# Two-layer streaming encoder on one core: RWKV's output norm by tile, layer vectors loaded early, feed-forward weights in a ring of four, root first, products of constants on TensorE

## The chip, the core and the metric

The kernel runs on one core of a Trainium2 chip. Its engines are TensorE (PE, matrix products), VectorE (DVE), ScalarE (ACT), GpSimd (POOL) and SyncE (SP, which issues the transfers). The metric is the time of one execution on the device, in microseconds; lower is better. TensorE's clock has two levels here, 1.2 and 2.4 GHz; the profile's column PEclk is the granted share, 0.50 and 1.00.

## The reference, cut

Two layers over 528 tokens (16 meta tokens and 512) of width 1024. A layer is: half-step feed-forward (width 2816), three token mixers side by side (RWKV-7, mLSTM, sparse attention) with a gated merge, second half-step feed-forward. Each has an RMS norm in front and behind.

The second piece below is from `_rwkv7_mixer`, behind its scan.

```python
def _rms_norm(x, g):
    xf = x.astype(jnp.float32)
    y = xf * lax.rsqrt(jnp.mean(xf * xf, axis=-1, keepdims=True) + NORM_EPS)
    return (y * g.astype(jnp.float32)).astype(x.dtype)

def _swiglu(x, w_in, w_out):
    gate, up = jnp.split(x @ w_in, 2, axis=-1)
    return (jax.nn.silu(gate) * up) @ w_out
...
    mean = jnp.mean(y, axis=-1, keepdims=True)
    var = jnp.mean((y - mean) ** 2, axis=-1, keepdims=True)
    y = (y - mean) * lax.rsqrt(var + RW_GN_EPS)
    y = y * gn_gain.astype(f32).reshape(RW_HEADS, RW_HEAD) + gn_bias.astype(f32).reshape(RW_HEADS, RW_HEAD)
    y = y + jnp.sum(r_h * k_h * r_k.astype(f32), axis=-1, keepdims=True) * v_h
    return (y.reshape(bsz, t_len, BRANCH_W) * gate.astype(f32)).astype(p.dtype)
...
    for l in range(DEPTH):
        g = norm_gain[l]
        h = h + 0.5 * _rms_norm(_swiglu(_rms_norm(h, g[0]), ffn_w_in[l, 0], ffn_w_out[l, 0]), g[1])
        u = _rms_norm(h, g[2])
        ...
        h = h + _rms_norm(mixed, g[3])
        h = h + 0.5 * _rms_norm(_swiglu(_rms_norm(h, g[4]), ffn_w_in[l, 1], ffn_w_out[l, 1]), g[5])
```

## The kernel before

Activations stand transposed: feature tiles of 128 partitions by T = 528 tokens (`h` is the residual, KD = 8 tiles; `fo` the output of the last sub-layer, 8 tiles). Two halves of H2 = 264 tokens fill a pair of PSUM banks. An exact product in f32r is three matmuls (`exact`, L141 to L143): weights and activations are split into a high and a low part, high by high, low by high, high by low. The split of weights is made on the chip: ACT copies W to `W_high` (L150), POOL subtracts (`W_low`, L156).

The program is a sequence of phases, each a block of one instruction stream per engine, with all semaphores cleared between two; the streams are ordered by hand with semaphores. Each layer of a loop runs: `phase_params` (13 small transfers of the layer's vectors, two transposes, one copy to `prm`), feed-forward 0, RWKV, sparse attention, mLSTM, merge, feed-forward 1. Behind both layers come a last normalisation (`phase_post_norm`) and the output.

A phase behind a sub-layer begins with a **lead** (class `Lead`). It does the post norm of the sub-layer before, the residual and the sums for the next norm:

- `tensor_post`: column sums of the squares `ssq` over 128 partitions, as matmuls with the squares as weights and one column of `ones` (L355; f32, so each is two instructions of the trace: 20 rows); `factor` on DVE (L381 to L384) turns sums into reciprocals, `root` on ACT (L329) takes the square root, `spread_out` (L362) spreads the factors over partitions on PE.
- for each of 8 tiles k: DVE scales `fo` (L400) and adds it to `h` (L401), ACT makes `u_high` (L338) and the squares (L341), DVE makes `u_low` (L395); PE does the products of tile k for the first two weight tiles (12 matmuls) and the column sums of the squares (L355, 10 rows).
- a second `factor`, `root`, `spread_out`, and the copy to `rs` (L412), by which the feed-forward scales its outputs.

In RWKV's phase (`later` false) the products wait for the second factor: the scaled `h` is made behind it (L423, L348, L417), so that no product lies between the sums.

The feed-forward (`phase_ffn`) has two weight buffers of 8 blocks (128 x 1024). Tile (i, s) is 48 matmuls: gate and up for two hidden tiles each i, s = 0 to 3, PSUM pair s. A buffer is split again when PE is through with the tile before the last (`tile_done`). DVE takes tiles out of PSUM (L603, L608), multiplies by ACT's Silu (L572) and splits the result (L616, L618). The second half of the phase, 8 output tiles of 22 blocks, goes through the same buffers in 24 units. ACT and DVE put out each output tile and its squares (`Out`, L469, L470, L478).

RWKV's output norm is the last block of `phase_rwkv` (L1301 to L1352). It goes step by step over all four tiles of y: sums, mean off, squares, sums of squares, root, `widen` (four DVE copies, L813) and spread, scale, gain and bias, bonus, gate.

## Time and profile before

| | us |
|---|---|
| median of 3 runs | 3931.65 (3928.18 to 3960.33) |
| profiled execution, its own time | 3944.31 |
| its span | 3942.5 |
| TensorE busy | 3576.1, 91% |
| mean granted clock of TensorE | 0.934 |

The page of the profile lists busy time per engine. The view of stretches gives, for a piece of the span, busy time per engine and the granted clock. The timeline lists instructions in order, equal ones merged into one row with their count, and in brackets how long the engine was idle before and what ended it. PE lists a matmul from start to modelled end, so the pitch of a row of matmuls is its length by its count.

### The profile page before, as it was taken

How to read it: one execution, taken by the hardware profiler on the slowest of the kernel's cores; microseconds unless marked ns; L12 is line 12 of the kernel's file. 1: busy time of each engine (PE TensorE's matmuls, PEld its weight loads, DVE VectorE, ACT ScalarE, POOL GpSimd, SP SyncE). 2: the span in 40 equal slices, each digit the busy share in tenths (PEclk: the TensorE clock that was granted, in tenths of full speed). 3: DMA queues.
4: the chain of work that ended last, by engine and by line, in shares of the span. 5: the costliest groups of instructions: out<-in, count | busy, mean ns of one | idle time of the engine just before them, and what ended most of it. 6: DMA issues, size and time to landing. Idle time of an engine off the chain costs nothing. (4 is left out here: it accounts for less than half of the span.)

```text
span 3942.5 us, 76414 instructions
## 1 busy us (share of the span) xinstructions
PE 3576.1 (91%) x32360; PEld 3360.8 (85%) x32360; DVE 1567.9 (40%) x2554; ACT 1066.0 (27%) x1830; POOL 1053.0 (27%) x576
## 2 busy tenths in 40 slices
PE   6999999887979898999979998988789789989998
PEld 5999898775758798999979998987667678989997
DVE  3442244444764123443134413344457631234422
ACT  2222252112453112222222223421125521132221
POOL 2443234110002112344324442341100112124442
PEclk9999899997999898999979998999889889989998
DMA  1333222001101331233223332210011103213332
GB/s 55 91 90 91 70 61 53 3 3 35 49 17 35 81 81 54 75 90 88 78 61 90 90 90 57 69 34 3 2 49 41 35 13 98 73 54 91 90 91 70
DMA packets 458793, 236.77 MB, mean 60 GB/s; under 512 B 15230, under 2 KB 456844, under 8 KB 458524
## 3 DMA queue, kind: packets, MB, share of 16 engines
q1 hardware_dynamic: 458524, 232.90, 21.3%
q8 instruction: 203, 3.33, 0.4%
q14 instruction: 66, 0.54, 0.0%
HBM read 230.50 MB, written 2.10 MB: 59 GB/s over the span
## 5 line engine op out<-in xcount | busy, mean ns | idle before, releaser
L141 PE MATMUL PS<-u_high,W_high 128*128 128x264 f32 x3328 | 965.8, 290 | 46.3 <-POOL W_low L665 23.6
L142 PE MATMUL PS<-u_low,W_high 128*128 128x264 f32 x3328 | 956.3, 287 | 0.0
L143 PE MATMUL PS<-u_high,W_low 128*128 128x264 f32 x3328 | 955.9, 287 | 0.0
L156 POOL TENSOR_TENSOR W_low<-W,W_high 128x1024 fp32r<-128x1024 f32 (+1 forms) x272 | 632.6, 2326 | 1086.4 <-ACT W_high L150 1086.4
L141 PEld LDWEIGHTS PS<-u_high,W_high 128*128 128x128 f32 x3328 | 640.2, 192 | 48.2 <-POOL W_low L665 23.8
L142 PEld LDWEIGHTS PS<-u_low,W_high 128*128 128x128 f32 x3328 | 641.4, 193 | 0.5
L143 PEld LDWEIGHTS PS<-u_high,W_low 128*128 128x128 f32 x3328 | 638.0, 192 | 0.0
L150 ACT ACTIVATE W_high<-W 128x1024 fp32r<-128x1024 f32 (+1 forms) x272 | 281.6, 1036 | 1126.9 <-PE PS L143 1114.7
L141 PE MATMUL PS<-u_high,dW_high 128*128 128x264 f32 (+1 forms) x1536 | 466.5, 304 | 19.3 <-POOL dW_low L1416 7.9
L1416 POOL TENSOR_TENSOR dW_low<-dW,dW_high 128x512 fp32r<-128x512 f32 x128 | 206.5, 1620 | 947.2 <-ACT dW_high L1411 947.0
L142 PE MATMUL PS<-u_low,dW_high 128*128 128x264 f32 (+1 forms) x1536 | 442.9, 288 | 0.0
L143 PE MATMUL PS<-u_high,dW_low 128*128 128x264 f32 (+1 forms) x1536 | 442.8, 288 | 0.0
L142 PE MATMUL PS<-hidden_low,W_high 128*128 128x264 f32 x1408 | 401.0, 285 | 0.0
L143 PE MATMUL PS<-hidden_high,W_low 128*128 128x264 f32 x1408 | 399.2, 284 | 0.0
L141 PE MATMUL PS<-hidden_high,W_high 128*128 128x264 f32 x1408 | 398.9, 283 | 0.0
L141 PEld LDWEIGHTS PS<-u_high,dW_high 128*128 128x128 f32 (+1 forms) x1536 | 296.4, 193 | 36.4 <-issue 21.6
L142 PEld LDWEIGHTS PS<-u_low,dW_high 128*128 128x128 f32 (+1 forms) x1536 | 296.6, 193 | 1.9
L143 PEld LDWEIGHTS PS<-u_high,dW_low 128*128 128x128 f32 (+1 forms) x1536 | 294.8, 192 | 0.0
L478 DVE TENSOR_TENSOR ssq<-ssq 128x528 f32<-128x528 f32 x36 | 89.5, 2487 | 443.6 <-ACT ssq L469 443.6
L141 PEld LDWEIGHTS PS<-hidden_high,W_high 128*128 128x128 f32 x1408 | 265.3, 188 | 0.0
L143 PEld LDWEIGHTS PS<-hidden_high,W_low 128*128 128x128 f32 x1408 | 265.0, 188 | 0.0
L142 PEld LDWEIGHTS PS<-hidden_low,W_high 128*128 128x128 f32 x1408 | 264.3, 188 | 0.0
(339 smaller groups left out, 5403.3 us busy)
## 6 DMA issues: line engine op xcount, KB each, us to landing
W<-in_ffn_w_in SPq DMA_DIRECT2D x176, 512.0 KB, 4.0
dW<-in_w_in SPq DMA_DIRECT2D x188, 256.0 KB, 2.9
W<-in_ffn_w_out SPq DMA_DIRECT2D x64, 512.0 KB, 4.0
W<-in_w_in SPq DMA_DIRECT2D x32, 512.0 KB, 5.4
W<-in_ffn_w_out SPq DMA_DIRECT2D x32, 384.0 KB, 3.5
W_branch<-in_w_branch SPq DMA_DIRECT2D x16, 768.0 KB, 5.1
W<-in_w_out SPq DMA_DIRECT2D x16, 512.0 KB, 4.2
xt<-in_x SPq DMA_DIRECT2D x4, 512.0 KB
```

The source lines that it names most:

```text
L141: nc.tensor.matmul(dst, wh, xh, start=first, stop=False)
L142: nc.tensor.matmul(dst, wh, xl, start=False, stop=False)
L143: return nc.tensor.matmul(dst, wl, xh, start=False, stop=final)
L150: nc.scalar.activation(WH[:, w, 0:k], W[:, w, 0:k], ACT.Copy).then_inc(S("high"), 1)
L156: g.tensor_tensor(WL[:, w, 0:k], W[:, w, 0:k], WH[:, w, 0:k].bitcast(F32), ALU.subtract).then_inc(S("split"), 1)
L478: nc.vector.tensor_tensor(ssq[:, 2], ssq[:, 2] if m > 1 else ssq[:, 0], ssq[:, m % 2], ALU.add).then_inc(S("added"), 1)
L1416: g.tensor_tensor(self.WL[:, r], self.W[:, r], self.WH[:, r].bitcast(F32), ALU.subtract).then_inc(S("d_split"), 1)
```

## The change

1. **Layer vectors.** `phase_params` is gone. A class `Params` issues the 13 transfers within `phase_start` (layer 0) and within feed-forward 1 (the next layer), behind its first eight weight loads on SP; PE transposes them and DVE copies them to `prm` at the end of that phase.
2. **Root first.** ACT takes the square root of a constant at the start of each lead, which puts the table load there; DVE's `memset` of `rq` waits for it. The first weight splits stand behind the root, not ahead of it.
3. **Sums.** Column sums of `Lead` use 64 columns of ones, not 1. In the feed-forward the sums of the eight squares are `ones` by squares (2 x 264 columns), so that they arrive spread over the partitions; reciprocal and root are taken on the 128 x 528 tile `rs`. PE waits only until DVE has read the sums (`sums_read`).
4. **Products of constants.** `occupy` (ones by ones, 128 columns, to a bank not in use): 4 behind the first sums, 12 (feed-forward) or 8 (RWKV) behind the spread, 1 behind each sum of RWKV's lead and 4 behind the last, 8 behind RWKV's second spread, 7 at the end of feed-forward 0 and of the merge.
5. **Ring of four.** The feed-forward's weights go through four buffers of 4 blocks (128 x 512): 88 units for the first half of the phase, 48 for the second, where 44 and 24 were.
6. **RWKV's output norm by tile.** Subtraction of the mean in one step from PSUM, squares, bonus, spread and gates interleaved tile by tile; `wide` and its copies are gone (the spread reads `rq` broadcast to 64 columns, two halves). Gain with bonus, and bias with gate, are each one operation.
7. Two `memset` of RWKV's `s3` go from DVE to POOL.

```diff
+        class Params:
...
+            def load(self, sp, l):
+                pa, pb = self.pa, self.pb
+                come = S("params_come")
+                sp.dma_start(pa[0:48, :], norm_gain[ds(l, 1)].rearrange("a g (k p) -> (a g k) p", p=P)).then_inc(come, 16)
...
+            def turn(self, pe, bank):
+                pe.wait_ge(S("params_come"), 13 * 16)
+                nc.tensor.transpose(bank[:, 0:G_MU], self.pa[0:G_MU, :], ident[0:G_MU, 0:G_MU])
+                n = G_END - G_MU
+                nc.tensor.transpose(bank[:, G_MU:G_END], self.pb[0:n, :], ident[0:n, 0:n]
+                                    ).then_inc(S("params_turned"), 1)
+            def out(self, v, bank):
+                v.wait_ge(S("params_turned"), 1)
+                nc.vector.tensor_copy(prm[:], bank[:, 0:G_END]).then_inc(S("params"), 1)
...
+                    firstp.load(sp, 0)
...
+                    pe.wait_ge(ev["dve_to_pe"], KD - 3)
+                    firstp.turn(pe, PS[:, 0])
...
+                nc.scalar.activation(self.rq[:, 0], ones[:, 0:8], ACT.Sqrt).then_inc(S("table"), 1)
                 self.root(act, 0)
+                if between:
+                    between(act, None)
...
-                self.root(act, 1)
-                if not self.later:
+                if self.later:
+                    act.wait_ge(S("recip"), 2)
+                    nc.scalar.activation(rs[:], rs[:], ACT.Sqrt).then_inc(S("rs"), 1)
...
-                    ins = nc.tensor.matmul(self.sums[0:n, j:j + 1], src[:, t0:t0 + n], ones[:, 0:1],
+                    ins = nc.tensor.matmul(self.sums[0:n, 64 * j:64 * j + 64], src[:, t0:t0 + n], ones[:, 0:64],
...
+                for _ in range(count):
+                    nc.tensor.matmul(self.idle, ones[:], ones[:], start=True, stop=True)
+
             def tensor_post(self, pe):
                 self.column_sums(ssq[:, 2], True, False)
                 self.column_sums(ssq[:, 1], False, True).then_inc(S("summed"), 1)
+                self.occupy(pe, 4)
                 self.spread_out(pe, 0)
+                self.occupy(pe, 12 if self.later else 8 if self.pre is not None else 0)
...
-                self.column_sums(self.ring[k % 2], k == 0, k == KD - 1).then_inc(S("h_summed"), 1)
+                if not self.later:
+                    self.column_sums(self.ring[k % 2], k == 0, k == KD - 1).then_inc(S("h_summed"), 1)
+                    self.occupy(pe, 1 if k < KD - 1 else 4)
+                    return
+                for a in range(2):
+                    last = nc.tensor.matmul(self.wide_sums[:, a], ones[:], self.ring[k % 2][:, a * H2:(a + 1) * H2],
+                                            start=k == 0, stop=k == KD - 1)
+                last.then_inc(S("h_summed"), 1)
...
             def vector(self, v):
                 own = Chain(v, S("norm_own"))
+                v.wait_ge(S("table"), 1)
                 own(nc.vector.memset(self.rq[:], 1.0))
...
+                if self.later:
+                    own(nc.vector.tensor_scalar(halves(rs[:]), self.wide_sums, 1.0 / D_MODEL, EPS, ALU.mult, ALU.add))
+                    v.sem_inc(S("sums_read"), 1)
+                    nc.vector.reciprocal(rs[:], rs[:]).then_inc(S("recip"), 1)
+                    return
                 self.factor(v, own, 1)
                 v.wait_ge(S("spread"), 2)
-                if self.later:
-                    nc.vector.tensor_copy(rs[:], self.spread).then_inc(S("rs"), 1)
-                    return
...
-                W, WH, WL = weight_buffers(st, KD)
+                R = 4
+                W, WH, WL = (sb(st, n, [P, R, 4, P], dt) for n, dt in (("W", F32), ("W_high", F32R), ("W_low", F32R)))
...
+                PARTS = tuple((k0, min(4, KF - k0)) for k0 in range(0, KF, 4))
+                first = [(t, k0) for k0 in (0, 4) for t in range(2)] + [(t, k0) for t in (2, 3) for k0 in (0, 4)]
...
+                        if nextp:
+                            nextp.load(sp, sp.snap(1 - l))
...
+                                for q in range(2):
+                                    load(8 * i + 2 * s + q, (2 * s + q) % R, wi[:, 4 * q:4 * q + 4, ds(c, P)])
...
-                        pe.wait_ge(S("split"), 4)
+                                n = 2 * (k // 4) + s
+                                if k % 4 == 0:
+                                    pe.wait_ge(S("split"), n + 1 + R)
+                                product(s, n, k % 4, k)
                             lead.tensor_square(pe, k)
-                        lead.spread_out(pe, 1)
                         pe.sem_inc(dve_evac, 4)
+                        pe.wait_ge(S("sums_read"), 1)
                         tile(0, 2)
-                        pe.wait_ge(S("rs"), 1)
...
+                            last.then_inc(S("unit_done"), 1)
+                        if nextp:
+                            pe.wait_ge(S("out_put"), KD - 3)
+                            nextp.turn(pe, PS[:, 0])
+                        else:
+                            pe.wait_ge(S("out_put"), KD - 3)
+                            lead.occupy(pe, 7)
...
-                        for s in range(2):
-                            high_part(act, s, 16, W, WH, s, KD)
-                        lead.scalar(act)
-                        high_part(act, 2, 32, W, WH, 0, KD)
+                        def first_high(act, k):
+                            for n in {None: (0, 1), 0: (2,), 1: (3,), 5: (4,), 6: (5,), 7: (6,)}.get(k, ()):
+                                high(n, n // R, n % R, 4)
+
+                        lead.scalar(act, first_high)
+                        high(7, 1, 3, 4)
                         silu(0, 0)
-                        high_part(act, 3, 32, W, WH, 1, KD)
...
+                        if nextp:
+                            v.wait_ge(S("gs"), 1)
+                            nextp.out(v, PS[:, 0])
...
+                    g.memset(s3[:], 1.0).then_inc(S("starts"), 1)
-                    own(nc.vector.memset(s3[:], 1.0))
...
                     lead.spread_out(pe, 1)
+                    lead.occupy(pe, 8)
                     dense.leading_pair(pe, S("u_low"))
...
+                    def bonus_out(m):
+                        v.wait_ge(S("bonus"), m + 1)
+                        nc.vector.tensor_tensor(halves(s1[:, m]), pair(B_PAIR[m]), halves(v_[:, m]), ALU.mult
+                                                ).then_inc(S("bonus_out"), 1)
+
+                    def scaled(m):
+                        v.wait_ge(S("var_spread"), m + 1)
+                        nc.vector.tensor_tensor(y[:, m], y[:, m], spread(S_PAIR[m]), ALU.mult
+                                                ).then_inc(S("scaled"), 1)
+
+                    def joined(m):
+                        v.wait_ge(S("scaled"), m + 1)
+                        v.wait_ge(S("bonus_out"), m + 1)
+                        stt(out=y[:, m], in0=y[:, m], scalar=col(G_GG, m), in1=s1[:, m], op0=ALU.mult, op1=ALU.add
+                            ).then_inc(S("joined"), 1)
+
+                    def gated(m):
+                        v.wait_ge(S("joined"), m + 1)
+                        v.wait_ge(S("gates"), m + 1)
+                        stt(out=halves(y[:, m]), in0=halves(y[:, m]), scalar=col(G_GB, m), in1=pair(G_PAIR[m]),
+                            op0=ALU.add, op1=ALU.mult).then_inc(S("gated"), 1)
...
+                        v.wait_ge(S("sum_y"), m + 1)
+                        stt(out=halves(y[:, m]), in0=pair(m), scalar=-1.0 / 64, in1=halves(y[:, m]),
+                            op0=ALU.mult, op1=ALU.add).then_inc(S("centred"), 1)
...
+                    bonus_out(0)
+                    bonus_out(1)
+                    scaled(0)
+                    bonus_out(2)
+                    joined(0)
+                    bonus_out(3)
+                    gated(0)
+                    for m in range(1, 4):
+                        scaled(m)
+                        joined(m)
+                        gated(m)
...
+                    def spread_out(m):
+                        for j, (t0, n) in enumerate(ST_):
+                            for b in range(2):
+                                c = 8 * j + 2 * m + b
+                                last = nc.tensor.matmul(spread(S_PAIR[m])[64 * b:64 * b + 64, t0:t0 + n],
+                                                        rq[0:n, c:c + 1].broadcast_to([n, 64]), ident[0:n, 0:n],
+                                                        start=True, stop=True)
...
+                        sums(y[:, m], half_ones[:], m, "sum_y")
+                    for m in range(4):
+                        squares(m)
+                    bonus(0)
+                    bonus(1)
+                    pe.wait_ge(S("var_rsqrt"), 1)
+                    spread_out(0)
+                    pe.wait_ge(S("bonus_out"), 1)
+                    bonus(2)
+                    pe.wait_ge(S("bonus_out"), 2)
+                    bonus(3)
+                    gates(0)
+                    pe.wait_ge(S("bonus_out"), 3)
+                    spread_out(1)
+                    pe.wait_ge(S("bonus_out"), 4)
+                    gates(1)
+                    for m in (2, 3):
+                        pe.wait_ge(S("scaled"), m - 1)
+                        spread_out(m)
+                        pe.wait_ge(S("gated"), m - 1)
+                        gates(m)
...
-            run(phase_params, l)
```

ACT at the start of a feed-forward, before (`hid` are the squares, the branches at phase starts left out):

```order
L150 ACT_TABLE_LOAD
L150 ACTIVATE W_high<-W 128x1024 x2
L329 ACT_TABLE_LOAD
L329 ACTIVATE rq<-rq 128x8
L338 ACTIVATE u_high<-h,prm 128x528
L341 ACTIVATE hid<-h 128x528
```

And in the change:

```order
L322 ACT_TABLE_LOAD
L322 ACTIVATE rq<-ones 128x8
L319 ACTIVATE rq<-rq 128x8
L614 ACTIVATE W_high<-W 128x512 x2
L331 ACTIVATE u_high<-h,prm 128x528
L334 ACTIVATE hid<-h 128x528
L614 ACTIVATE W_high<-W 128x512
```

The table for the root is loaded ahead of everything, the root comes ahead of the splits, and these are half as wide.

PE at the start of a feed-forward before, from the sums of the post norm to the first products:

```order
L355 MATMUL PS<-ones,ssq 128x1 x4
L355 MATMUL PS<-ones,ssq 16x1
L355 MATMUL PS<-ones,ssq 128x1 x4
L355 MATMUL PS<-ones,ssq 16x1
L362 MATMUL PS<-ident,rq 128x128 x4
L362 MATMUL PS<-ident,rq 128x16
L141 MATMUL PS<-u_high,W_high 128x264
L142 MATMUL PS<-u_low,W_high 128x264
```

Further on, the last products of tile k = 0, its sums and the first products of k = 1:

```order
L142 MATMUL PS<-u_low,W_high 128x264
L143 MATMUL PS<-u_high,W_low 128x264
L355 MATMUL PS<-ones,hid 128x1 x4
L355 MATMUL PS<-ones,hid 16x1
L141 MATMUL PS<-u_high,W_high 128x264
L142 MATMUL PS<-u_low,W_high 128x264
```

In the change, the same two pieces:

```order
L351 MATMUL PS<-ones,ssq 128x64 x4
L351 MATMUL PS<-ones,ssq 16x64
L368 MATMUL PS<-ones 128x128 x4
L358 MATMUL PS<-ident,rq 128x128 x4
L358 MATMUL PS<-ident,rq 128x16
L368 MATMUL PS<-ones 128x128 x12
L141 MATMUL PS<-u_high,W_high 128x264
L142 MATMUL PS<-u_low,W_high 128x264
```

```order
L141 MATMUL PS<-u_high,W_high 128x264
L142 MATMUL PS<-u_low,W_high 128x264
L143 MATMUL PS<-u_high,W_low 128x264
L384 MATMUL PS<-hid,ones 128x264 x2
L141 MATMUL PS<-u_high,W_high 128x264
L142 MATMUL PS<-u_low,W_high 128x264
```

The constants stand between sums and spread and between spread and products; the ten narrow sums of a tile are two wide matmuls.

PE in RWKV's output norm before, from the spread of tiles 2 and 3 to its end (`gup` are the gate's weights):

```order
L187 MATMUL PS<-ident,wide 128x16
L187 MATMUL PS<-ident,wide 128x128 x4
L187 MATMUL PS<-ident,wide 128x16
L1351 MATMUL PS<-rw_s_1,half_ones 128x264 x8
L1351 MATMUL PS<-pj_rw,gup 128x264 x8
```

And in the change, from the bonus sums of tiles 0 and 1 to the gates of tile 1:

```order
L1430 MATMUL PS<-rw_s_1,half_ones 128x264 x4
L1450 MATMUL PS<-ident,rw_rq 64x128 x8
L1450 MATMUL PS<-ident,rw_rq 64x16 x2
L1430 MATMUL PS<-rw_s_1,half_ones 128x264 x4
L1430 MATMUL PS<-pj_rw,gup 128x264 x2
L1450 MATMUL PS<-ident,rw_rq 64x128 x8
L1450 MATMUL PS<-ident,rw_rq 64x16 x2
L1430 MATMUL PS<-pj_rw,gup 128x264 x2
```

The spread of tile 0 no longer waits for a widened copy, and bonus sums and gates lie between the spreads.

## Rows read from the trace of the kernel before

**Rows 1.** The page's busy times, TensorE: us, share of the span, instructions.

```profile
PE 3576.1 (91%) x32360; PEld 3360.8 (85%) x32360; DVE 1567.9 (40%) x2554; ACT 1066.0 (27%) x1830; POOL 1053.0 (27%) x576
```

**Rows 2.** Stretches (windows): start:end us, length, busy per engine, granted clock.

```profile
core 0: us, PE busy (x) PEld busy (x) DVE busy (x) ACT busy (x) POOL busy (x), PEclk, DMA share, GB/s
34.56:87.08 52.52, 40.33 (x216) 39.38 (x217) 18.95 (x34) 17.80 (x25) 6.98 (x3) 1.00 0.15 41
1548.02:1593.61 45.59, 34.02 (x217) 33.05 (x217) 18.97 (x34) 16.64 (x24) 6.98 (x3) 0.69 0.17 47
1593.61:1599.40 5.79, 5.79 (x26) 5.79 (x27) 4.41 (x4) 1.30 (x2) 2.38 (x1) 0.50 0.35 101
1599.40:1968.10 368.70, 368.70 (x3048) 368.70 (x3046) 126.63 (x112) 84.99 (x99) 148.71 (x64) 1.00 0.30 87
1984.30:2030.44 46.14, 34.10 (x217) 33.13 (x217) 18.96 (x34) 17.82 (x25) 6.98 (x3) 0.68 0.17 47
3494.15:3538.08 43.93, 30.61 (x216) 29.62 (x217) 18.97 (x34) 16.64 (x24) 6.99 (x3) 0.77 0.17 49
462.68:496.97 34.29, 24.62 (x121) 23.51 (x121) 16.01 (x31) 10.01 (x16) 3.70 (x3) 0.50 0.24 62
890.90:935.40 44.50, 27.68 (x112) 24.02 (x112) 24.96 (x33) 2.20 (x2) 0.00 (x0) 0.69 0.00 0
```

**Rows 3.** Timeline (start us, length us), second feed-forward, layer 0: its lead.

```profile
1548.14 3.88 PE L355 MATMUL PS<-ones,ssq 128*128 128x1 f32 x20 [2.08 <-PEq L161]
...
1555.46 1.28 ACT L329 ACT_TABLE_LOAD   x1
...
1556.75 0.21 ACT L329 ACTIVATE rq<-rq 128x8 f32<-128x8 f32 x1
...
1557.01 2.61 PE L362 MATMUL PS<-ident,rq 128*128 128x128 f32 x10 [4.99 <-ACT rq L329]
...
1560.40 0.71 DVE L401 TENSOR_TENSOR h<-h,fo 128x528 f32<-128x528 f32 x1
...
1562.38 0.76 DVE L395 SCALAR_TENSOR_TENSOR u_low<-h,prm,u_high 128x528 fp32r<-128x528 f32 x1
```

**Rows 4.** Timeline, last normalisation: the same 20 column sums at full clock.

```profile
3913.97 2.29 PE L355 MATMUL PS<-ones,ssq 128*128 128x1 f32 x20 [2.21 <-PEq L161]
```

**Rows 5.** Timeline, parameter phase of each layer and the lead behind it.

```profile
26.69 0.35 SPq L277 DMA_DIRECT2D pa<-in_norm_gain  x1
...
34.56 0.07 DVE L388 MEMSET rq<- 128x16 f32 x1 [0.69 <-PEq L161]
...
1974.82 0.36 SPq L277 DMA_DIRECT2D pa<-in_norm_gain  x1
...
1984.30 0.07 DVE L388 MEMSET rq<- 128x16 f32 x1 [0.69 <-PEq L161]
```

**Rows 6.** Timeline, RWKV phase, layer 0: the 80 column sums of its lead.

```profile
475.76 15.54 PE L355 MATMUL PS<-ones,rw_s 128*128 128x1 f32 x80 [2.21 <-ACT rw_s L341]
```

**Rows 7.** Timeline, RWKV output norm, layer 0.

```profile
890.93 2.93 DVE L1308 TENSOR_SCALAR rw_s<-PS 128x528 f32<-128x528 f32 x4 [6.25 <-PE PS L1351]
...
898.47 7.84 PE L174 MATMUL PS<-half_ones,rw_s 128*128 128x2 f32 x40 [7.58 <-ACT rw_s L1342]
...
907.40 3.00 DVE L813 COPY wide<-rw_rq 128x640 f32<-128x640 f32 x4 [0.36 <-ACT rw_rq L1344]
...
908.27 10.23 PE L187 MATMUL PS<-ident,wide 128*128 128x128 f32 x40 [1.96 <-DVE wide L813]
...
928.46 3.83 PE L1351 MATMUL PS<-pj_rw,gup 128*128 128x264 f32 x16 [3.15 <-DVEq L1333]
```

**Rows 8.** Costs of single forms: a line's own view, then groups by shape.

```profile
L616 DVE CAST hidden_high<-hid x88: 435/2426/2637, 88.6 to 3785.1; 128x528 f32 x88
...
L1416 POOL TENSOR_TENSOR dW_low<-dW,dW_high 128x512 fp32r<-128x512 f32 x128 | 206.5, 1620 | 947.2 <-ACT dW_high L1411 947.0
...
L1411 ACT ACTIVATE dW_high<-dW 128x512 fp32r<-128x512 f32 x192 | 119.0, 626 | 141.1 <-PE PS L143 130.2 <-DMA dW<-in_w_in 10.6
```

290 lines of the change are left out of this document (135 added, 155 removed).

## Prediction

> **What bounds the kernel now.** I read the page's busy times first: TensorE is busy for 91% of the span [rows 1]. That says where to look, not what can be won, so I went on to the view of stretches [rows 2]. There the kernel falls into two kinds. The long piece of a feed-forward behind its lead (1599.40 to 1968.10) is full: PE is busy for all of its 368.7 us, 3048 matmuls, 0.121 us each, at 2.4 GHz. Nothing of the change can shorten that piece; it can only break it. The other kind are leads and RWKV's output norm. The four feed-forward leads take 52.5, 45.6, 46.1 and 43.9 us, with 217 matmul rows where the full piece would have put 360 or more; RWKV's lead takes 34.3 (here DVE's first memset to the first product), its output norm 44.5. Their granted clock is 0.50 to 0.77. (The first lead shows 1.00 only because the profile has no clock record ahead of 77 us; its 216 rows are as slow as the others'.) Even behind a lead the clock stays low for a while: 1593.61 to 1599.40 has 26 matmuls in 5.79 us, 0.223 each. So the kernel is bound by PE, and in its leads by a PE that waits, then works at half the clock.
>
> The timeline of a lead shows why [rows 3]. 20 column sums of one column take 3.88 us; the same 20 at full clock take 2.29 [rows 4]. Then ACT splits two weight tiles, loads the table of the root (1.28), and only then takes the root; the spread begins 5.0 us after the sums end. Behind it, DVE and ACT need two operations on `h` and two for high and low before the first product.
>
> **The change, part by part.** I add up against the profiled execution, 3944.3 us with its span of 3942.5; it lies 12.7 above the median of the three runs, so I take the difference over to the median.
>
> *Layer vectors.* From the first transfer of the parameter phase to the lead behind it: 26.69 to 34.56, and 1974.82 to 1984.30 [rows 5]. The 13 transfers now lie under the transposes at the start, and under the full piece of feed-forward 1 (13 times some 0.35 us on SP, behind eight weight loads; the ninth load is needed only when four units are through). What stays is about 0.4 us to enter the next phase. Gain 7.5 + 9.1 = 16.6, say **16.5**. Two transposes and a copy come behind the phase's last product, hidden under ACT's last 1.4 us of output. If they weren't: 1 us.
>
> *Feed-forward leads.* New length at full clock, entered from a busy phase: sums 2.3 [rows 4], reciprocal and root 0.9, spread of 10 rows at 0.112 = 1.1, fo and h 1.4, high 0.7, low 0.8 [rows 3]: the first product at 7.3. The 12 constants (24 rows at 0.112 = 2.7) lie under the last four of these. Then eight tiles: 12 products at 0.121 and four rows of 264 columns. 16 such rows took 3.83, 0.24 each [rows 7], with a start among them; I take 0.223. A tile is 2.34 us, eight are 18.7; reading the sums 0.9. Together 27.0. Now the cost that the code hides: POOL's split (1.25 to 1.6 a unit [rows 8]) used to be over when DVE began on `h`. Root first moves DVE some 7 us forward, and seven splits now fall into the tile loop. DVE's cast of `hidden`, 0.435 alone, has a median of 2.43 us beside POOL [rows 8]. In the lead, `h` add (L401) and low (L395) read two SBUF tensors each, and I expect them to wait for POOL as that cast does. Bounds: 0, and seven times 1.6 = 11. DVE needs 2.0 to 2.2 of each 2.34 us, which swallows 2 to 3 of it; I take +3: **30.0**. From a cold start (layer 0 and 1, feed-forward 0): sums 3.9, four constants 1.7 (they cover the root), spread 2.2, then 3.2 to the first product, 18.7, 0.9 and 3: **33.7**, if the constants have the clock up when the products begin.
> The Trainium skill (GPSIMD Engine Reference, section Key points) says that GpSimd shares its SBUF interfaces with VectorE, in contention with instructions in a two-port mode or with two SBUF inputs. It speaks against this part; the cast agrees, and no row shows L401 or L395 beside POOL.
> Gains: 52.5 - 33.7, 45.6 - 30.0, 46.1 - 33.7, 43.9 - 30.0 = 60.7. To this the low clock behind the leads: half of 3.6, 5.8, 5.9 and 3.4 us = 9.3. Sum **70**.
>
> *RWKV's lead.* New: sums 2.3, root 0.9, spread 1.1, first `h` and square 2.1; then eight tiles at DVE's pace of 1.42 (its sums and constant 1.25 on PE at full clock [rows 4]) to the last sum, 11.0; root and spread 2.0, scale, high and low 2.2: 21.7. The same POOL collision adds up to 4.8 (three splits), I take 3: 24.7 instead of 34.3, and 3 us of low clock behind it half back. **11 each, 22**. Before, the 80 sums alone took 15.54 [rows 6]. The memsets that go to POOL were done before the sums came.
>
> *RWKV's output norm.* Before: 890.9 to 935.3 on DVE, 44.4, in which DVE works 25 us and PE and DVE take turns: squares only after all is centred, 40 sum rows 7.84, widen 3.00 (its first part ahead of the spread), spread 10.23, then gain, bonus, gate [rows 7]. After: DVE has 4 bonus terms, 4 centrings, 0.7 for the variance and 16 operations of 0.70 to 0.80 [rows 3, 7], 18.7 us in all, and starts during the sums of y, some 3 us ahead of 890.9. What it must wait for: squares of the last tile and its sums (to about 895), root and the first spread (898). From there 14 operations are left (two bonus products come ahead of the spread), 10.4 us: end at 909, gain 26. If PE stays at 1.2 GHz: sums of squares till 898.6, bonus 3.5, then four spreads, two bonus and four gates 19: end at 922, gain 13. The spread by halves is not in the trace; if its two halves follow each other it costs 0.8 to 1.5 more for each tile, and this makes the same 13 to 26. PE does little for some 4 us in the middle, so one drop of the clock is likely. I take **22 each, 44**.
>
> *Costs.* 272 waits of PE for a unit become 544. In the full piece a tile's first row costs no more than some 0.01 us extra: **-2.5**. Seven constants at a phase's end: 14 rows at 0.112 = 1.6, under ACT's last output. What hides them is that output; gone, they cost 1.6 x 4.
>
> Sum: 16.5 + 70 + 22 + 44 - 2.5 = **150**. From the median, 3931.65 - 150 = about **3781**.
>
> **Rivals.**
> *The clock doesn't come up.* The gain of the leads rests on 2.4 GHz. The stretches show that dense products bring it (26 at 0.223, then 0.121) and that sums of one column don't hold it: RWKV's lead has PE busy for 24.6 of 34.3 us and a clock of 0.50. Products of constants are not in the trace. If they count for nothing: feed-forward leads at low clock, sums 3.9, constants 1.7, spread 2.2, constants 5.1, eight tiles of 4.4 and 0.9 = 49, loses 8 over four; RWKV's lead with the added constants 37, loses 6; norm 26, vectors 16.5, costs -2.5. Gain 26: **3905**. Against it: wide sums are ordinary matmuls without a pause between them and the products.
> The Trainium skill (TensorE: Matmul & The Clock Gate, section What's actually happening) says the default is the throttled clock and that activity releases it. By that rule the constants work.
> *The collision is small.* No waits for POOL in leads and the norm at its best: +12 +6 +8, gain 176: **3756**.
> *The ring starves (slower).* A unit lasts PE 24 x 0.121 = 2.9 us. Its successor in the same buffer needs ACT 0.63 and POOL 1.25 to 1.6 [rows 8] and has three units, 8.7 us. To be slower, each of the 544 units would have to leave PE waiting for 0.28 us, as when a load were asked for too late or POOL held up by DVE for over 6 us. If each waits 0.4: 218 against 150, **4000**. The weights come at a transfer share of 0.30 [rows 2]; I hold it unlikely.
>
> **How the numbers follow.** Forecast 0.55, small collision 0.17, clock stays low (or only partly up, 3840 to 3905) 0.18, ring starves 0.03, and 0.07 for some other loss that leaves it between. Faster by over 1% means under 3892; within 1% is about what a measurement can't tell from no change. Of the clock rival a third lies above 3892: faster 0.90, same 0.07, slower 0.03. Range: down to the small collision and a little more of the leads, 3745; up to a clock that comes in half of the leads, 3840.
>
> **What would show it.** Right: the parameter phase gone and the first lead at 27; feed-forward leads of 27 to 34 us at a clock of 0.9 and more; `h` adds of 0.71 to 2 us, some beside POOL; the norm on DVE in 20 to 26 us from 890.9's counterpart; the full piece still 0.121 a matmul with no waits for W_low. Wrong: a lead with a clock of 0.50, 0.44 for a row of 264 columns, or waits of PE for POOL's split in the full piece.

## The result, and the profile after

The changed kernel takes 3792.78 us (median of 4 runs, 3787.12 to 3794.45), the kernel before beside it 3929.91 (3926.51 to 3960.33): a ratio of 0.9632, 95% interval 0.9583 to 0.9681. The prediction was 3781, its range 3745 to 3840. The two profiled executions stand at 3944.31 and 3792.09, spans 3942.5 and 3790.4: a difference of 152.1 us between the spans, which is what the traces can be asked about.

The page after: TensorE's busy time (compare [rows 1]) and its granted clock in 40 slices, in tenths.

```profile
PE 3536.4 (93%) x32526; PEld 3310.6 (87%) x32526; DVE 1459.7 (39%) x2531; ACT 1129.5 (30%) x2113; POOL 1148.0 (30%) x852
...
PEclk9999999998998899999999999999989889999998
```

Stretches after, columns as in [rows 2]: the first lead, second feed-forward of layer 0 (lead, then all that stands behind it), the loop's back edge, the two other feed-forward leads, both RWKV leads, both RWKV output norms. A lead begins here with its first column sum and ends with the first product behind its loop (RWKV: the first product).

```profile
26.89:60.37 33.48, 31.30 (x191) 28.47 (x191) 20.62 (x29) 15.65 (x26) 8.94 (x7) 1.00 0.28 80
1487.74:1518.93 31.19, 28.74 (x190) 26.27 (x191) 20.60 (x29) 15.79 (x26) 8.91 (x7) 0.95 0.31 87
1518.93:1890.93 372.00, 372.00 (x3073) 372.00 (x3073) 106.29 (x118) 102.94 (x167) 171.59 (x129) 1.00 0.30 87
1890.93:1896.67 5.74, 0.43 (x4) 0.20 (x3) 0.30 (x1) 1.20 (x2) 0.00 (x0) 0.98 0.03 9
1896.67:1929.22 32.55, 30.09 (x190) 27.36 (x190) 20.61 (x29) 15.87 (x26) 8.93 (x7) 0.90 0.31 83
3354.71:3385.87 31.16, 28.71 (x191) 26.18 (x191) 20.61 (x29) 15.79 (x26) 8.92 (x7) 0.95 0.30 87
...
434.76:458.57 23.81, 23.23 (x182) 20.53 (x183) 16.38 (x29) 10.14 (x17) 6.81 (x5) 1.00 0.33 90
2303.60:2328.70 25.10, 24.58 (x182) 22.02 (x183) 15.98 (x29) 10.19 (x17) 6.36 (x5) 0.93 0.32 85
...
847.21:871.32 24.11, 22.84 (x168) 18.11 (x168) 17.79 (x27) 2.81 (x5) 0.00 (x0) 0.93 0.00 1
2715.38:2742.50 27.12, 24.47 (x169) 19.40 (x169) 17.80 (x27) 3.45 (x6) 0.00 (x0) 0.87 0.00 1
```

(The last of them ends with the next phase's first matmul, 1 us behind the norm.) Against the rows of before this gives the account of the 152.1 us; predicted is the term of the sum:

| part | before | after | gain | predicted |
|---|---|---|---|---|
| layer vectors, start and loop's edge | first sums at 34.68; edge 16.07 | first sums at 26.89; edge 5.58 | 18.3 | 16.5 |
| four feed-forward leads | 52.4, 45.5, 46.0, 43.8 | 33.5, 31.2, 32.6, 31.2 | 59.3 | 60.7 |
| what stands behind these, 3072 matmuls each | 373.7, 374.7, 374.8, 373.7 | 372.2, 372.2, 372.1, 372.1 | 8.3 | 9.3 - 2.5 |
| two RWKV leads | 34.3, 34.2 | 23.8, 25.1 | 19.6 | 22 |
| two RWKV output norms (by the same DVE operation behind each) | | | 25.8 + 24.4 | 44 |
| all else (balance of several, see below) | | | -3.6 | 0 |

How a new lead runs, second feed-forward of layer 0 (timeline: start us, length us), against [rows 3]:

```profile
1487.74 2.54 PE L351 MATMUL PS<-ones,ssq 128*128 128x64 f32 x20 [0.83 <-PEq L147]
...
1490.21 2.05 PE L368 MATMUL PS<-ones 128*128 128x128 f32 x8
...
1490.88 0.21 ACT L319 ACTIVATE rq<-rq 128x8 f32<-128x8 f32 x1 [1.83 <-DVE rq L396]
...
1492.05 2.16 PE L358 MATMUL PS<-ident,rq 128*128 128x128 f32 x10
...
1494.98 0.71 DVE L414 TENSOR_TENSOR h<-h,fo 128x528 f32<-128x528 f32 x1
...
1496.97 0.76 DVE L408 SCALAR_TENSOR_TENSOR u_low<-h,prm,u_high 128x528 fp32r<-128x528 f32 x1
...
1498.38 1.17 DVE L414 TENSOR_TENSOR h<-h,fo 128x528 f32<-128x528 f32 x1
...
1499.38 1.30 POOL L541 TENSOR_TENSOR W_low<-W,W_high 128x512 fp32r<-128x512 f32 x1 [0.39 <-ACT W_high L614]
1499.48 1.77 DVE L408 SCALAR_TENSOR_TENSOR u_low<-h,prm,u_high 128x528 fp32r<-128x528 f32 x1
...
1501.30 0.39 PE L141 MATMUL PS<-u_high,W_high 128*128 128x264 f32 x1 [0.89 <-DVE u_low L408]
```

The root no longer waits behind splits and a table. The collision with POOL is there, as forecast, and small: one add of `h` takes 1.17 instead of 0.71, one low part 1.77 instead of 0.76, and TensorE waits once in the loop (0.89). The other tiles come at 2.35 us, 12 products and 4 sums of 264 columns, with no wait.

### The profile page after: what moved, and what is told of

The parts are those of the page before. It is cut to its first block and busy times, and to the rows that moved or that the text cites. A ratio compares the mean times of both kernels' runs of the same rounds, so it can differ in the third digit from the quotient of the medians.

```text
span 3790.4 us, 79640 instructions
## 1 busy us (share of the span) xinstructions
PE 3536.4 (93%) x32526; PEld 3310.6 (87%) x32526; DVE 1459.7 (39%) x2531; ACT 1129.5 (30%) x2113; POOL 1148.0 (30%) x852
## 5 line engine op out<-in xcount | busy, mean ns | idle before, releaser
L541 POOL TENSOR_TENSOR W_low<-W,W_high 128x512 fp32r<-128x512 f32 (+1 forms) x544 | 721.0, 1327 | 908.2 <-ACT W_high L614 908.2
L141 PE MATMUL PS<-u_high,W_high 128*128 128x264 f32 x3328 | 955.2, 287 | 32.7 <-POOL W_low L718 23.2
L142 PE MATMUL PS<-u_low,W_high 128*128 128x264 f32 x3328 | 944.7, 284 | 0.0
L143 PE MATMUL PS<-u_high,W_low 128*128 128x264 f32 x3328 | 944.4, 284 | 0.0
L141 PEld LDWEIGHTS PS<-u_high,W_high 128*128 128x128 f32 x3328 | 628.6, 189 | 38.3 <-POOL W_low L718 23.4
L614 ACT ACTIVATE W_high<-W 128x512 fp32r<-128x512 f32 (+1 forms) x544 | 335.6, 619 | 1005.4 <-PE PS L143 966.7
L142 PEld LDWEIGHTS PS<-u_low,W_high 128*128 128x128 f32 x3328 | 629.1, 189 | 1.2
L143 PEld LDWEIGHTS PS<-u_high,W_low 128*128 128x128 f32 x3328 | 625.9, 188 | 0.0
L141 PEld LDWEIGHTS PS<-u_high,dW_high 128*128 128x128 f32 (+1 forms) x1536 | 296.4, 193 | 32.7 <-issue 21.6
L493 DVE TENSOR_TENSOR ssq<-ssq 128x528 f32<-128x528 f32 x36 | 63.1, 1752 | 464.2 <-ACT ssq L484 464.2
```

What stands on the lines that cost most here:

```text
L141: nc.tensor.matmul(dst, wh, xh, start=first, stop=False)
L142: nc.tensor.matmul(dst, wh, xl, start=False, stop=False)
L143: return nc.tensor.matmul(dst, wl, xh, start=False, stop=final)
L493: nc.vector.tensor_tensor(ssq[:, 2], ssq[:, 2] if m > 1 else ssq[:, 0], ssq[:, m % 2], ALU.add).then_inc(S("added"), 1)
L541: g.tensor_tensor(WL[:, r, 0:nk], W[:, r, 0:nk], WH[:, r, 0:nk].bitcast(F32), ALU.subtract).then_inc(S("split"), 1)
L614: nc.scalar.activation(WH[:, r, 0:nk], W[:, r, 0:nk], ACT.Copy).then_inc(S("high"), 1)
```

## The experiments

Each is the changed kernel with the edit shown, timed beside the kernel before. Where a text says slower or faster, it compares the run's median with the changed kernel's 3792.78. The kernel before stood at 3934.1 to 3937.8 beside the experiments, 4 to 8 us above the 3929.9 beside the result: a difference of a few us between two such medians says little. The lead lengths below are measured from first sum to the first product as above. No run takes back the ring of four or the early layer vectors alone; what they are worth is read from the traces.

### Without constants

```diff
             def occupy(self, pe, count):
-                for _ in range(count):
-                    nc.tensor.matmul(self.idle, ones[:], ones[:], start=True, stop=True)
+                return
...
-                    for _ in range(7):
-                        nc.tensor.matmul(PS[:, 0, 0:P], ones[:], ones[:], start=True, stop=True)
```

> The changed kernel with every product of constants left out (in the leads, in front of the second spread, at the ends of the phases); the sums stay 64 columns wide. They only warm TensorE, so nothing of the result is left out. Theory A, the constants bring the clock up: the four feed-forward leads (31.2 to 33.5 us in the changed kernel) run in part at a clock of 0.50, each 5 to 12 us longer, and RWKV's two leads, whose eight tiles wait for DVE, 4 to 8 us longer: the whole 30 to 60 us slower than the changed kernel, 3823 to 3853. Theory B, the dense products and the wide sums bring it by themselves: leads within 2 us of the changed kernel's, the whole 3785 to 3800.

Measured: 3815.87 us, ratio 0.9698 (0.9661 to 0.9734). That is 23 us slower than the changed kernel, less than theory A asked and more than B. The stretches say where: an RWKV lead, then the feed-forward lead that suffered most.

```profile
433.83:468.21 34.38, 27.52 (x120) 23.57 (x120) 16.36 (x29) 9.86 (x17) 5.86 (x5) 0.50 0.23 62
...
1495.42:1529.49 34.07, 28.78 (x159) 26.04 (x159) 20.32 (x29) 15.45 (x26) 8.90 (x7) 0.75 0.28 80
```

RWKV's leads are at 34.4 and 34.2, where they were before the change [rows 2], all at half the clock. The feed-forward leads are at 32.8, 34.1, 33.0 and 31.2, that is -0.7, +2.9, +0.5 and 0.0 us against those with constants: the dense products bring the clock up inside the lead. The constants are worth 23 us of the 137 (22 between the two traces), and 20 of these lie in the two leads whose tile loop has no product in it.

### Without constants, sums one column wide

```diff
-                    ins = nc.tensor.matmul(self.sums[0:n, 64 * j:64 * j + 64], src[:, t0:t0 + n], ones[:, 0:64],
+                    ins = nc.tensor.matmul(self.sums[0:n, 64 * j:64 * j + 1], src[:, t0:t0 + n], ones[:, 0:1],
```

> As the one before, and the column sums of both post norms and of RWKV's lead are one column wide again (as in the kernel before), so that only the order, the ring and the direct sums of the feed-forward lead are left of the change there. Theory A: RWKV's lead falls back to the clock of 0.50 that it had before and takes 30 us or more, the feed-forward leads lose some more: 3830 to 3880. Theory B (the clock comes by the products alone in the feed-forward lead, and RWKV's lead waits for DVE at either clock): feed-forward leads below 36, RWKV's below 27, the whole below 3810.

Measured: 3808.13 us, ratio 0.9677 (0.9641 to 0.9713); 8 us faster than the run before it.

```profile
434.29:465.01 30.72, 23.86 (x120) 22.74 (x121) 16.37 (x29) 9.97 (x17) 5.85 (x5) 0.52 0.27 69
```

RWKV's leads take 30.7 and 31.4, as theory A had it; the feed-forward leads 30.8 to 33.3 and the whole below 3810, as B had it. Where the clock is low anyway, 64 columns only cost: 34.4 against 30.7. Wide sums without constants are worse than neither. In the four feed-forward leads the two edits together buy nothing: without both they take 127.5 us in sum, in the changed kernel 128.4. Constants with sums one column wide were not run, so it is open whether RWKV's leads need the wide sums as well.

### The old order of root, table and splits

```diff
-                nc.scalar.activation(self.rq[:, 0], ones[:, 0:8], ACT.Sqrt).then_inc(S("table"), 1)
-                self.root(act, 0)
-                if self.pre is None:
-                    return
+                act.sem_inc(S("table"), 1)
                 if between:
                     between(act, None)
+                self.root(act, 0)
+                if self.pre is None:
+                    return
```

> The changed kernel with the old order on ScalarE in each lead: the two splits of weights first, then the load of the root's table, then the root; constants, sums and ring as changed. Theory A, the order is worth its own length on the path: table 1.28 and two splits of 0.63, less what lies under the sums (2.5 to 4.5): each of six leads 1.5 to 2.5 us longer, the whole 8 to 15 slower, 3801 to 3808. Theory B, the wait that it leaves makes the clock fall inside the lead: feed-forward leads 5 us and more longer, 3815 and up. Theory C, the constants behind the sums hide it: within 2 us.

Measured: 3810.58 us, ratio 0.9683 (0.9647 to 0.9719), 18 slower: above the 3801 to 3808 of theory A and below the 3815 of B. The feed-forward leads are 1.2, 2.5, 3.0 and 2.5 us longer (sum 9.1), near A; but in the last three of them the clock is low for 6.8, 17.1 and 10.2 us where the changed kernel has 3.4, 6.8 and 3.4, so a part of the 9.1 is B's, and how much isn't separated. RWKV's leads are 5.5 and 4.7 longer. Timeline of RWKV's lead, layer 0:

```profile
439.62 0.63 ACT L1525 ACTIVATE dW_high<-dW 128x512 fp32r<-128x512 f32 x1 [4.71 <-DMA dW<-in_w_in]
...
442.20 1.28 ACT L319 ACT_TABLE_LOAD   x1
...
443.76 2.61 PE L358 MATMUL PS<-ident,rq 128*128 128x128 f32 x10 [4.22 <-ACT rq L319]
```

ACT sits 4.71 us waiting for the weights to land, with the root queued behind it: there the old order made the root wait for a transfer, which none of the theories had. The 4.22 us that TensorE waits here brought the clock down for 6.8 us only (4.41 us and 6.8 in layer 1): it was back before the first square's sums, behind 10 rows of spread and most of 16 of constants, and then it held.

### More constants

```diff
+                    for _ in range(10):
+                        nc.tensor.matmul(PS[:, 2, 0:P], ones[:], ones[:], start=True, stop=True)
                     pe.wait_ge(S("h_squares"), 1)
```

and the same with 8 behind these 40 sums, 28 at the start of the merge, twice 8 at the start of the sparse attention (DSA) phase and 6 ahead of the root in RWKV's norm.

> The changed kernel with more constants where TensorE still waits at a clock of 0.50: 10 and 8 (0.22 us each at full clock) around the 40 sums of mLSTM's output norm, 28 in the 8 us between that norm and the first product of the merge, 8 and 8 at the start of the DSA phase, 6 ahead of the root in RWKV's norm. If constants bring the clock up as well as in the leads: mLSTM's sums 7.8 to 4.5 us, its spread 10.2 to 7, merge's first 5 us halved, the DSA start 3 to 5 shorter: 8 to 12 a layer, the whole 3770 to 3777. If the 28 run at 0.50 they take 12 us instead of 6 and make the merge wait 4 us a layer: 3793 to 3800.

Measured: 3785.66 us, ratio 0.9615 (0.9578 to 0.9651), between the two theories. Around mLSTM's norm and the start of the merge the trace gains 7 us in layer 0 and 4.6 in layer 1. It loses 1.3 in each of RWKV's norms, where bonus and spread now queue behind the constants, and 1.7 and 2.2 at the DSA starts. And RWKV's lead in layer 0, which the edit does not touch, takes 33.46 instead of 23.81. Its timeline, and two stretches, the whole lead and its part at low clock:

```profile
439.76 1.28 POOL L1534 TENSOR_TENSOR dW_low<-dW,dW_high 128x512 fp32r<-128x512 f32 x1 [3.09 <-ACT dW_high L1529]
440.13 1.47 DVE L414 TENSOR_TENSOR h<-h,fo 128x528 f32<-128x528 f32 x1
...
442.46 1.32 PE L351 MATMUL PS<-ones,rw_s 128*128 128x64 f32 x10 [1.12 <-ACT rw_s L334]
...
434.47:467.93 33.46, 32.05 (x182) 28.63 (x183) 17.08 (x29) 10.09 (x17) 6.62 (x5) 0.69 0.24 64
...
444.40:464.90 20.50, 20.50 (x95) 18.30 (x95) 7.63 (x14) 4.06 (x7) 0.03 (x1) 0.50 0.10 25
```

The same place in the changed kernel:

```profile
440.42 0.76 DVE L414 TENSOR_TENSOR h<-h,fo 128x528 f32<-128x528 f32 x1
...
441.91 1.32 PE L351 MATMUL PS<-ones,rw_s 128*128 128x64 f32 x10 [0.28 <-ACT rw_s L334]
```

The chain in this lead: the weights land later, so POOL's first split starts 5.29 us behind the lead's first sum instead of 4.58; it meets the first add of `h`, the add takes twice as long, TensorE's wait for the first square grows from 0.28 to 1.12, and behind it the clock is 0.50 for 20.5 us. It came back behind the last sums, in the rows of constants and of the second spread. The collision that costs 0.7 us by itself costs 9.7 through the clock. In layer 1 of the same trace the first add takes 0.75, the wait is 0.34 and the lead 23.81.

### Splits ahead of the tile loop

```diff
-                            for n in {None: (0, 1), 0: (2,), 1: (3,), 5: (4,), 6: (5,), 7: (6,)}.get(k, ()):
+                            for n in {None: (0, 1, 2, 3), 5: (4,), 6: (5,), 7: (6,)}.get(k, ()):
```

> The changed kernel with four instead of two units split behind the root in each feed-forward lead, so that POOL is through with them before the tile loop. In the changed kernel's trace POOL's splits of units 2 and 3 stretch one add of h (L414) from 0.71 to 1.17 and one low part (L408) from 0.76 to 1.77, and TensorE then waits 1.2 us in the second tile. Theory A, this is the collision: the loop of eight tiles falls from 21.15 to about 20 us in each of four leads, but POOL now meets the first add of h, up to 0.8 later for the first product: 0 to 1 us a lead, the whole within 4 us of the changed kernel (3789 to 3796). Theory B, the later start leaves TensorE waiting longer behind its constants and the clock falls there: 3 us and more a lead, above 3800.

Measured: 3794.67 us, ratio 0.9640 (0.9624 to 0.9656): no change against the changed kernel. The loop falls from 21.15 to 20.0 in two of the four leads, as theory A has it for the collision; in one of the others, at 1487, the first product waits instead (2.82 us; 0.70 in the changed kernel). The loops of these two take 21.3 and 21.6, each with a dip of the clock of 3.4 us in it, a little of theory B.

```profile
1495.79 1.77 DVE L408 SCALAR_TENSOR_TENSOR u_low<-h,prm,u_high 128x528 fp32r<-128x528 f32 x1
...
1497.61 0.59 PE L141 MATMUL PS<-u_high,W_high 128*128 128x264 f32 x1 [2.82 <-DVE u_low L408]
```

So the collision in a feed-forward lead is worth 1.2 us, can be moved and not removed this way.

### Column sums in the feed-forward leads

```diff
-                for a in range(2):
-                    last = nc.tensor.matmul(self.wide_sums[:, a], ones[:], self.ring[k % 2][:, a * H2:(a + 1) * H2],
-                                            start=k == 0, stop=k == KD - 1)
-                last.then_inc(S("h_summed"), 1)
+                self.column_sums(self.ring[k % 2], k == 0, k == KD - 1).then_inc(S("h_summed"), 1)
...
-                        pe.wait_ge(S("sums_read"), 1)
                         tile(0, 2)
+                        pe.wait_ge(S("rs"), 1)
                         tile(0, 3)
```

and the second root, spread and copy of the kernel before.

> The changed kernel with the feed-forward leads' second normalisation done as before: column sums by block of tokens (here 64 columns wide), a second root, spread and copy, instead of sums over ones that come out spread. Constants, order and ring as changed. Theory A, these leads win by having less on TensorE's and the root's path: a tile's sums 1.25 instead of 1.0 us and the second root and spread 2.5: each lead 3 to 6 us longer, the whole 12 to 24 slower, 3805 to 3817. Theory B, they win because sums of 264 columns hold the clock: the clock falls in the loop, leads 10 us and more longer, above 3830.

Measured: 3806.75 us, ratio 0.9669 (0.9653 to 0.9686), 14 slower. The loops take 24.7 instead of 21.15, all four alike, at the clock of the changed kernel (0.95, as there):

```profile
1485.44:1520.20 34.76, 32.55 (x249) 30.20 (x249) 19.84 (x31) 17.46 (x29) 9.64 (x8) 0.95 0.29 81
```

Theory A: 58 rows more in each lead and a root and spread to wait for. Sums of 264 columns win by their number and by coming out spread, not by the clock.

### RWKV's output norm undone

The last block of RWKV's phase as in the kernel before, all else changed.

> The changed kernel with RWKV's output norm as it was before, all else as changed. Theory A, the trace's own difference (25.8 us in layer 0, 24.4 in layer 1) is the norm's share: 46 to 54 slower, 3839 to 3847. Theory B, what stands behind it takes part of it back (the start of the DSA phase runs at a clock of 0.50 behind either norm): 35 to 45.

Measured: 3836.54 us, ratio 0.9740 (0.9724 to 0.9757), 44 slower. The number is that of theory B. Its trace has the norms at 25.8 and 24.6 us more, and behind them 2.3 us in layer 0 and 0.7 in layer 1 are given back, all of it in the DSA phase, as B had it (by the same DVE operations in both traces). RWKV's second lead in this trace is one at low clock (33.2 us, behind a wait of 0.93), 8.1 us longer than in the changed kernel, and its own time, 3844.8, is the highest of the four; the others lie 8 to 9.5 below. Without these 8.1 the spans differ by 44.6, beside the 44 of the medians. So the norm by tile saves 50 us in the norm and some 47 with what stands behind it; the rest down to 44.6 is mostly the last normalisation, 3.0 us shorter in this trace, which the edit doesn't touch.

### Constants around mLSTM's norm, 12 in RWKV's lead

```diff
-                self.occupy(pe, 12 if self.later else 8 if self.pre is not None else 0)
+                self.occupy(pe, 12 if self.pre is not None else 0)
...
                     pe.wait_ge(S("h_squares"), 1)
                     pe.wait_ge(S("sums_read"), 1)
                     token_sums(lambda m: hq[:, m], ones[:, 0:1], 1).then_inc(S("h_sums"), 1)
+                    for _ in range(8):
+                        nc.tensor.matmul(PS[:, 2, 0:P], ones[:], ones[:], start=True, stop=True)
```

with the 10 ahead of the sums and the 28 ahead of the merge.

> The changed kernel with constants added only where they paid: 10 and 8 around the sums of mLSTM's output norm, 28 ahead of the merge; none in RWKV's norm and at the DSA start, where they made DVE and the first sums wait; and 12 instead of 8 behind the first spread of RWKV's lead. There the clock fell in one lead of the run before, behind a wait of TensorE of 1.12 us instead of 0.28, when the weights landed 0.4 us later and POOL's split held up the first add of h (1.47 us instead of 0.76); that lead took 33.5 us instead of 23.8. If both readings are right: RWKV's leads 23.8 to 24.5 in both layers, 7 to 9 us less around each mLSTM norm, the whole 3774 to 3780. If the cause of the fall is another, one of the two leads is again 30 and more: 3782 to 3790.

Measured: 3774.83 us (3773.25 to 3777.99), ratio 0.9586 (0.9570 to 0.9602). This is the fastest kernel of the study, 18 us below the changed one, the whole and RWKV's leads as both readings had them. Around mLSTM's norms and the start of the merge the trace gains 6.9 us in layer 0 and 4.6 in layer 1, less than the 7 to 9 each that were expected; together that is 11.5 of the 17.1 us between the spans, and another 3.1 lie in the last normalisation, which the edit doesn't touch. mLSTM's output norm, 40 sums and 40 rows of spread, in the changed kernel:

```profile
1222.67 7.81 PE L160 MATMUL PS<-ones,cv 128*128 128x1 f32 x40 [2.69 <-ACT cv L2196]
...
1232.51 10.23 PE L173 MATMUL PS<-ident,ml_rq 128*128 128x128 f32 x40 [2.03 <-DVE ml_rq L2146]
```

and here:

```profile
1222.99 5.00 PE L160 MATMUL PS<-ones,cv 128*128 128x1 f32 x40 [0.27 <-ACT cv L2202]
...
1231.49 6.56 PE L173 MATMUL PS<-ident,ml_rq 128*128 128x128 f32 x40
```

RWKV's leads, layer 0 and 1:

```profile
434.74:458.75 24.01, 23.71 (x191) 21.35 (x191) 16.56 (x29) 10.08 (x17) 6.82 (x5) 1.00 0.35 89
2297.90:2322.14 24.24, 23.94 (x190) 21.42 (x190) 16.80 (x29) 10.20 (x17) 6.82 (x5) 1.00 0.33 88
```

The first add of `h` is again late in both (0.94 and 1.19 us), but the longer row of constants covers it: TensorE has no wait, and the clock holds.

### Constants in RWKV's leads alone

```diff
-                self.occupy(pe, 4)
+                rwkv = self.pre is not None and not self.later
+                self.occupy(pe, 4 if rwkv else 0)
                 self.spread_out(pe, 0)
-                self.occupy(pe, 12 if self.later else 8 if self.pre is not None else 0)
+                self.occupy(pe, 8 if rwkv else 0)
```

and without the 7 at the end of the merge.

> The changed kernel with constants left only in RWKV's two leads and at the end of the feed-forward ahead of each; none in the four feed-forward leads and at the end of the merge. Without any constants the feed-forward leads took 31.2 to 34.1 us against 31.2 to 33.5 with them, RWKV's 34.3 against 23.8 and 25.1, and the whole was 23 slower. Theory A, all of the constants' worth lies in RWKV's leads: feed-forward leads as without constants, RWKV's 24 to 25, the whole 3790 to 3798. Theory B, their worth is spread over both kinds: 3800 to 3810.

Measured: 3805.10 us (3799.74 to 3811.85), ratio 0.9666 (0.9645 to 0.9686): the number of theory B. The trace says otherwise: the feed-forward leads are at 33.6, 34.1, 33.1 and 31.2, near those without constants and in sum 3.5 us above the changed kernel's, and RWKV's leads, whose constants were kept, take 33.7 and 33.3, 18.0 more (the spans differ by 16.7). Both have a first add of `h` held up by POOL, 1.69 and 1.36 us, and a wait behind it, 1.22 and 0.88.

```profile
440.54 1.69 DVE L415 TENSOR_TENSOR h<-h,fo 128x528 f32<-128x528 f32 x1
...
442.96 1.32 PE L351 MATMUL PS<-ones,rw_s 128*128 128x64 f32 x10 [1.22 <-ACT rw_s L334]
```

The weights were not late here: POOL's first split starts 4.29 and 3.95 us behind the lead's first sum, earlier than in the changed kernel (4.58), and it is the second split that the add meets. What holds for both cases is when the add ends: 0.56 us behind the end of the split under which it began. So its price is what is left of a split when it begins, and a shift of some tenths of a us either way can bring it on. Why the splits fell badly in both layers of this trace is not shown.

### Fewer constants behind RWKV's first spread

```diff
-                self.occupy(pe, 12 if self.later else 8 if self.pre is not None else 0)
+                self.occupy(pe, 12 if self.later else 4 if self.pre is not None else 0)
```

> The changed kernel with 4 instead of 8 constants behind the first spread of RWKV's two leads and nothing else changed: TensorE then waits some 0.9 us longer for the first square, 1.2 instead of 0.28. Theory A, that wait is what the clock falls behind (so far it fell in the two leads with 0.93 and 1.12, not in ten with 0.74 and less): both leads fall to 0.50 and take 30 to 34 us instead of 24 to 25, the whole 12 to 20 slower, 3805 to 3813. Theory B, the fall has to do with something else and comes by chance: lead times 23 to 25 in at least one layer, the whole 3788 to 3802.

Measured: 3804.62 us (3794.98 to 3809.77), ratio 0.9658 (0.9639 to 0.9677). In the profiled execution both leads fall, as in theory A: 36.3 us behind a wait of 1.98, 33.9 behind one of 1.27. In layer 0 the first add of `h` was held up as well (1.56 us); in layer 1 it took 0.76, as in the changed kernel, and nothing but the missing constants makes the wait. The lowest run, 10 us below the others, may be one in which one lead kept its clock (its mean granted clock is 0.959, the others' 0.954 to 0.956); it has no trace.

```profile
2314.56 0.76 DVE L414 TENSOR_TENSOR h<-h,fo 128x528 f32<-128x528 f32 x1
...
2316.14 1.58 PE L351 MATMUL PS<-ones,rw_s 128*128 128x64 f32 x10 [1.27 <-ACT rw_s L334]
...
2308.91:2342.83 33.92, 32.52 (x175) 28.86 (x175) 16.37 (x29) 10.08 (x17) 6.81 (x5) 0.65 0.23 63
```

Over the traces of the changed kernel and of all runs with constants in RWKV's lead and the root first, that is sixteen leads: in the six with a wait of 0.88, 0.93, 1.12, 1.22, 1.27 and 1.98 us ahead of the first square's sums the clock then stayed at 0.50 for 20.5 us or more, in the ten with waits of 0.74 or less it didn't (only dips of 3.4 us nearer the lead's start). Two edits in opposite directions bear it out, 4 constants (both fall) and 12 (neither falls). They change the wait together with the row of constants ahead of it; that the wait counts, the row being equal, is shown by the twelve leads with 8 constants alone, of which the four with 0.88 and more fell and the eight with 0.74 and less did not. And a wait isn't enough by itself: in the old order one of over 4 us ahead of the spread cost 6.8 us of low clock, with rows without a pause behind it.

## Why the prediction was right, and where its terms were off

*Layer vectors, 16.5.* Right: 7.8 at the start, 10.5 at the loop's edge, 1.4 more than forecast there, presumably since the dropped phase's own entry and exit went with its transfers.

The sum of the gains, 150, lies 2 us from the trace's 152.1, and that is in part luck: by parts, with the low clock counted as the prediction did, the norm gave 6 more than put and "all else" 7 less.

*Feed-forward leads, 60.7.* The sum held (59.3), its parts did not, and they cancelled. The first product of a warm lead comes 10.0 us behind the first sum, not 7.3. The four constants and the spread ran partly at 1.2 GHz (2.05 and 2.16 us above; RWKV's lead of layer 0 has the same 8 and 10 rows at full clock in 1.16 and 1.41), behind the change of phase; and DVE does the second tile's scale and add ahead of the first low part. The loop with the reading of the sums takes 21.15, not 22.6: the collision was put at +3 and is 1.2. The Trainium skill (GPSIMD Engine Reference, section Key points) speaks against the edit with the interfaces that GpSimd and VectorE share; the trace agrees on the mechanism, 1.77 against 0.76 us, and on a far smaller price than a lead full of such waits.

*Low clock behind the leads and the ring, 9.3 and -2.5.* Net 8.3 against 6.8. The long pieces stand at 372.1 to 372.2 us for 3072 matmuls. Before, they had 3.4, 5.8, 5.8 and 3.4 us of low clock in them, half of which is 9.2, as put; so twice as many waits cost 0.9 us in all and not 2.5, some 0.2 a phase. Over 360 us inside the piece of feed-forward 1, layer 0, first before, then after, they cost nothing that shows:

```profile
1605.00:1965.00 360.00, 360.00 (x2976) 360.00 (x2975) 125.92 (x111) 83.39 (x97) 147.35 (x64) 1.00 0.30 88
...
1525.00:1885.00 360.00, 360.00 (x2977) 360.00 (x2976) 101.42 (x115) 100.42 (x164) 170.38 (x129) 1.00 0.31 89
```

The ring does not starve.

*RWKV's leads, 22.* The leads gave 19.6 in the profiled execution, and the low clock behind them, which the 22 counted too, 1.4 and 1.9 more: 22.9. Here lay the step that carried the risk, and in this execution luck: it took the clock as held by the wide sums and constants. It is held only if the first square comes in time, and where POOL's splits fall decides that. Where the clock falls a lead is 33.2 to 36.3 us, and at most 1 us of its gain is left. The 3 us put for the collision stand for neither outcome: 0.3 us where the wait stays short, some 10 where it doesn't.

*Output norm, 44.* 25.8 and 24.4, at the upper bound: the clock stayed up nearly throughout (0.93 and 0.87), and the spread by halves follows at 1.31 us a tile. Timeline after, layer 0: the first centring, the sums of squares, the first spread, the last gate.

```profile
848.38 0.71 DVE L1398 SCALAR_TENSOR_TENSOR fo<-PS,fo 128x528 f32<-128x528 f32 x1 [0.39 <-PE PS L1430]
...
850.85 4.43 PE L1438 MATMUL PS<-half_ones,rw_s 128*128 128x2 f32 x40
...
858.88 1.31 PE L1450 MATMUL PS<-ident,rw_rq 128*64 128x128 f32 x20
...
870.55 0.77 DVE L1392 SCALAR_TENSOR_TENSOR fo<-fo,prm,PS 128x528 f32<-128x528 f32 x1
```

*All else, 0.* It is -3.6, and -6.9 without the 3.3 us behind RWKV's leads. Three places make up most of it: the DSA phases behind the new norm take 2.3 and 0.7 us of its gain back; mLSTM's norm of layer 0 loses 2.9, where the clock was low for 37.5 us after the change and for two times 13.7 before; the end of the kernel, from the last feed-forward on, loses 1.6. Why the clock was low for longer at mLSTM's norm is not shown.

*From 150 to the median.* The traces differ by 152.1, the medians by 137. The profiled execution of before lies 14 us above the median shown beside the result, that of after 0.7 below its own. Taking the sum over to the median whole was the step that put the forecast 12 us low.

*The rivals.* "The clock doesn't come up" was priced at 3905. The kernel without constants shows it at 3816: the price took all four feed-forward leads as staying at 1.2 GHz, 49 us each, and they take 31 to 34, since the clock comes up again in their products (0.75 over the lead at 1495.42). For RWKV's leads it was right: at half the clock throughout, 34.4 us where 37 was put. By the Trainium skill (TensorE: Matmul & The Clock Gate, section What's actually happening), activity releases the throttle. The feed-forward leads agree; in the stretch from 444.40 TensorE was busy throughout, and the clock stayed at 0.50 for its 20.5 us.

## What to carry over

A wait on TensorE costs its own length, and, where the work behind it doesn't bring the clock back, half the pace of everything up to the next stretch that does; count both, and look for what makes that one wait vary. Fill it for its late case (four more constants cost 0.2 us in the lead and save 10), and only where it is: the same constants in front of work that was ready made it later. Sums of 64 columns without constants were the worst choice in RWKV's leads; the feed-forward leads, with their products, needed neither.

## What the runs showed of the hardware

- TensorE at 1.2 GHz with PE busy for all of a stretch of 20.5 us (95 rows of 64 and 128 columns, f32): the busy column alone doesn't tell whether the clock comes up. The same rows keep 2.4 GHz where the stretch is entered at 2.4 (the lead at 434.76, clock 1.00).
- A DVE add of two SBUF tensors, 0.71 us alone, took up to 1.84 beside POOL's subtraction; the low part (two SBUF inputs) 0.76 and up to 1.79. In the traces of the changed kernel and its ten variants every such add of more than 0.72 us (119) and every low part of more than 0.78 (107) ends 0.56 to 0.57 us behind the end of the POOL subtraction under which it began: it waits for that one to end. DVE's multiply with one input in PSUM took 0.69 to 0.71 each time, beside POOL or alone.
- The 20 rows of column sums in f32 take 2.54 us with 64 columns (the row at 1487.74) and 2.29 with one [rows 4], both at 2.4 GHz: 63 more columns cost 0.01 us a row.
